# Gate/up weights of a decoder layer split four blocks at a time in place of two, and the first projection blocks in passes

## What is computed

```
h   = rmsnorm(x, attn_norm)
qkv = h @ w_in                          # 1024 x 3072
q, k = rope(q), rope(k);  two causal mixers of 8 heads each, side by side
mixed = [rmsnorm(o_moba, g1), rmsnorm(o_dil, g2)]
x = x + mixed @ w_out                   # 1024 x 1024
h = rmsnorm(x, ffn_norm)
g, u = h @ w_gate, h @ w_up             # 1024 x 2816 each
x = x + (silu(g) * u) @ w_down          # 2816 x 1024
return rmsnorm(x, final_norm)
```

## Time and profile before

| | us |
|---|---|
| median of 3 runs (lowest, highest) | 296.89 (296.17, 297.11) |
| profiled execution, its own time | 296.56 |
| its span (first to last instruction) | 294.7 |
| TensorE busy | 284.1 (96% of the span) |
| VectorE busy | 264.3 (90%) |
| ScalarE busy | 190.0 (64%) |

### The profile page before, as it was taken

How to read it: one execution, slowest core, us unless ns; L and a number is a source line. 1 busy time by engine, 2 the same in 40 slices (tenths; PEclk the granted TensorE clock), 3 DMA queues, 4 the chain that set the end, 5 groups by cost and what they waited for, 6 DMA issues and landing times.

```text
span 294.7 us, 4123 instructions
## 1 busy us (share of the span) xinstructions
PE 284.1 (96%) x1396; PEld 232.4 (79%) x1396; DVE 264.3 (90%) x424; ACT 190.0 (64%) x323; POOL 21.5 (7%) x27
## 2 busy tenths in 40 slices
PE   8899999999999999999999999999999999999990
PEld 4688878888888888888887888888888888888870
DVE  3788999999798869799899999999999999988993
ACT  3887767846696629867566674748484848475524
POOL 0002000000131514200000000000000000000040
PEclk9999999999999999999999999999999999999998
DMA  7999616797867828695766587777657483223003
GB/s 242 392 420 365 212 38 212 218 290 210 274 201 206 322 83 270 201 301 182 221 257 250 210 256 277 246 283 213 249 161 304 126 335 75 109 48 131 2 0 142
DMA packets 29797, 62.87 MB, mean 213 GB/s; under 512 B 3792, under 2 KB 17104, under 8 KB 28368
## 3 DMA queue, kind: packets, MB, share of 16 engines
q1 hardware_dynamic: 27616, 61.03, 60.5%
q10 hardware_dynamic: 2160, 1.59, 1.7%
HBM read 55.72 MB, written 1.11 MB: 193 GB/s over the span
## 4 chain that ended last, share of the span: by engine, by line
PE 79%; DVE 9%; DMA 3%; issue 3%; ACT 2%; SPq 1%; POOL 0%; POOLq 0%; ACTq 0%
PE bank L587 25%; PE bank L588 24%; PE bank L589 24%; PE bank L664 2%; DMA room<-in_first 2%; DVE w_lo L1366 2%; DMA room<-room 1%; SPq L494 1%; PE bank L614 1%; DVE room L1409 1%; DVE o_lo L1422 1%; PE bank L637 1%; ACT w_hi L1034 1%; DVE o_lo L1429 1%; PE bank L597 1%
## 5 line engine op out<-in xcount | busy, mean ns | idle before, releaser
L587 PE MATMUL bank<-w_hi,x_hi 128*128 128x512 f32 x230 | 91.1, 396 | 1.6 <-DVE w_lo L1236 1.4
L589 PE MATMUL bank<-w_hi,x_lo 128*128 128x512 f32 x230 | 89.6, 390 | 0.0
L588 PE MATMUL bank<-w_lo,x_hi 128*128 128x512 f32 x230 | 89.6, 389 | 0.0
L587 PEld LDWEIGHTS bank<-w_hi,x_hi 128*128 128x128 f32 x230 | 43.2, 188 | 12.0 <-DVE w_lo L1236 1.8
L589 PEld LDWEIGHTS bank<-w_hi,x_lo 128*128 128x128 f32 x230 | 43.2, 188 | 9.2
L588 PEld LDWEIGHTS bank<-w_lo,x_hi 128*128 128x128 f32 x230 | 43.2, 188 | 8.5
L901 ACT ACTIVATE w_hi<-raw 128x1024 fp32r<-128x1024 f32 x33 | 33.7, 1050 | 9.8 <-issue 9.6
L1208 DVE TENSOR_TENSOR w_lo<-raw,w_hi 128x1024 fp32r<-128x1024 f32 x32 | 38.3, 1211 | 1.2 <-ACT w_hi L901 1.1
L1366 DVE TENSOR_TENSOR w_lo<-raw,w_hi 128x1024 fp32r<-128x1024 f32 x30 | 36.2, 1216 | 0.4
L1034 ACT ACTIVATE w_hi<-raw 128x1024 fp32r<-128x1024 f32 x29 | 30.2, 1051 | 0.0
L1045 ACT ACTIVATE rope_b<-bank,rstd 128x256 f32<-128x256 f32 x22 | 10.4, 471 | 30.6 <-PE bank L589 30.4
(11 more groups left out here) (149 smaller groups left out, 478.3 us busy)
## 6 DMA issues: line engine op xcount, KB each, us to landing
raw<-in_weights SPq DMA_DIRECT2D x74, 512.0 KB, 5.5
room<-in_weights SPq DMA_DIRECT2D x10, 1024.0 KB, 6.7
room<-room SPq DMA_DIRECT2D x76, 64.0 KB, 2.2
room<-in_first SPq DMA_DIRECT2D x3, 384.0 KB, 5.6
room<-in_first SPq DMA_DIRECT2D x1, 1024.0 KB, 9.1
xs<-in_x SPq DMA_DIRECT2D x2, 512.0 KB, 9.7
rot<-turned_sums SPq DMA_DIRECT2D x8, 128.0 KB, 4.1
room<-room ACTq DMA_DIRECT2D x12, 64.0 KB, 2.6
```

The source lines that it names most:

```text
L587: pe.matmul(dst, a_hi, w1, start=first, stop=False)
L588: pe.matmul(dst, a_hi, w2, start=False, stop=False)
L589: return pe.matmul(dst, a_lo, w1, start=False, stop=last)
```

## The change

It has three parts.

1. The gains are appended to the first load, 24 words a partition, which moves to its own room. The load from ScalarE's queue is gone. VectorE's first x_hi reads them where they land; POOL copies them to `gain`, and VectorE's first x_lo and ScalarE wait for that copy.
2. `first_block` becomes `early_block`, used for the even ones of the first eight blocks: 0, 2, 4 and 6.
3. In the chunk steps 3 to 9, the gate/up blocks of chunks 4 to 10 are split four at a time: two instructions of 2048 columns a chunk on each engine in place of four of 1024. Each raises `hi_ready` or `lo_ready` by 2.

In the later steps the first half of the next chunk's weights also stands ahead of the first down parts as a whole, where before only one pair did. The diff, cut to its core:

```diff
@@ build, room for the first loads
         for row_blocks, blocks in FIRST_LOADS:
-            width = len(row_blocks) * SEQ + len(blocks) * NB
-            first_dst.append(room[:, word:word + width])
+            start = word = word if first_dst else FIRST_ROOM
...
+            if not first_dst:
+                first_gain = room[:, word:word + G_END]
+                word += G_END
+            first_dst.append(room[:, start:word])
+            if len(first_dst) == 1:
+                word = 0
@@ TensorE
-            def first_block():
...
+            def early_block(i):
+
+                j, k = QKV_ORDER[i]
+                pe.wait_ge(*((xt_hi, k) if k else (x0_hi, 1)))
+                pe.wait_ge(hi_single, i // 2 + 1)
                 for s in range(SH):
+                    pe.matmul(bank[2 * j + s][:], x_hi[:, k, s * P:(s + 1) * P], w_hi[:, i, :], start=k == 0, stop=False)
+                pe.wait_ge(xt_lo, k + 1)
                 for s in range(SH):
+                    pe.matmul(bank[2 * j + s][:], x_lo[:, k, s * P:(s + 1) * P], w_hi[:, i, :], start=False, stop=False)
+                pe.wait_ge(lo_single, i // 2 + 1)
                 for s in range(SH):
+                    ins = pe.matmul(bank[2 * j + s][:], x_hi[:, k, s * P:(s + 1) * P], w_lo[:, i, :], start=False,
+                                    stop=k == KT - 1)
                 ins.then_inc(blk_done, 1)
...
-                if i == 0:
-                    first_block()
+                if i < SINGLES and i % 2 == 0:
+                    early_block(i)
                     return
@@ ScalarE
-            act.dma_start(gain[:], gains[:, :]).then_inc(in_gain, 16)
...
+            def gate_up_hi_half(c, h):
+
+                for j in (2 * h, 2 * h + 1):
+                    act.wait_ge(raw_full[j], ring_loads(STEP1_PAIR + j) + 16 * (c - 1))
+                act.wait_ge(gu_done, 2 * c - 2)
+                at = slice(QUAD * h, QUAD * h + QUAD)
+                act.activation(gate_up_at(c, QUAD * h, QUAD)[0], raw[:, at, :], ACT.Copy).then_inc(hi_ready, 2)
...
                 if c < NCH - 1:
-                    gate_up_hi(c + 1, 0)
+                    gate_up_hi_half(c + 1, 0)
                 else:
                     last_down_hi(0)
                 if c > 3:
                     down_first_hi(c - 2, 0)
                     down_first_hi(c - 2, 1)
-                if c < NCH - 1:
-                    gate_up_hi(c + 1, 1)
-                else:
+                if c == NCH - 1:
                     down_second_hi(c - 2)
                 hidden_hi(c - 1)
-                if c < NCH - 1:
-                    gate_up_hi(c + 1, 2)
-                else:
+                if c == NCH - 1:
                     last_down_hi(1)
                 evacuate(c, 0)
                 hidden_sums_hi(c - 1)
                 if c < NCH - 1:
-                    gate_up_hi(c + 1, 3)
+                    gate_up_hi_half(c + 1, 1)
                     down_second_hi(c - 2)
@@ VectorE
             def first_lo(k):
 
                 dve.wait_ge(*((xt_hi, k) if k else (x0_hi, 1)))
+                if k == 0:
+                    dve.wait_ge(in_gain, 1)
...
-            dve.wait_ge(in_gain, 16)
             dve.wait_ge(in_first[0], 16)
-            dve.tensor_scalar(x_hi[:, 0, :], first_x[0], gain[:, G_ATTN:G_ATTN + 1], None, ALU.mult).then_inc(x0_hi, 1)
+            dve.tensor_scalar(x_hi[:, 0, :], first_x[0], first_gain[:, G_ATTN:G_ATTN + 1], None, ALU.mult).then_inc(x0_hi, 1)
...
+            def gate_up_lo_half(c, h):
+
+                dve.wait_ge(hi_ready, STEP1_PAIR + (c - 1) * G_PAIRS + 2 * h + 2)
+                hi, lo = gate_up_at(c, QUAD * h, QUAD)
+                dve.tensor_tensor(lo, raw[:, QUAD * h:QUAD * h + QUAD, :], hi.bitcast(f32),
+                                  ALU.subtract).then_inc(lo_ready, 2)
...
-                gate_up_lo(c + 1, 0)
+                gate_up_lo_half(c + 1, 0)
                 if c > 3:
                     down_first_lo(c - 2, 0)
                     down_first_lo(c - 2, 1)
-                gate_up_lo(c + 1, 1)
                 hidden_sums(c - 1)
-                gate_up_lo(c + 1, 2)
                 multiply(c, 0)
                 turn_squares(c, 0)
                 hidden_lo(c - 1)
-                gate_up_lo(c + 1, 3)
+                gate_up_lo_half(c + 1, 1)
                 down_second_lo(c - 2)
@@ POOL
+            pool.wait_ge(in_first[0], 16)
+            pool.tensor_copy(gain[:], first_gain).then_inc(in_gain, 1)
```

More of the change, by code:

```diff
@@ L126 @@
 FRONT_W = 480
+FIRST_ROOM = 11 * NB
 PE_PLAN = {
@@ L240, in attention_tile, with build @@
     return 1, [4 * (u - 1) + 2 * i + r for i in range(2)], SEQ
-def build(nc, x, first, weights, gains, final_norm, table, out):
+def build(nc, x, first, weights, final_norm, table, out):
     f32, f32r, bf16 = mybir.dt.float32, mybir.dt.float32r, mybir.dt.bfloat16
@@ L937, in _ @@
             split_single(1)
-            act.wait_ge(in_gain, 16)
+            act.wait_ge(in_gain, 1)
             for b in range(2, SINGLES):
@@ L1703 @@
     x_turned = x[0].T.reshape(KT, P, SEQ)
-    first = np.concatenate([np.concatenate([x_turned[k] for k in row_blocks] + [qkv[b] for b in blocks], axis=1).reshape(-1)
-                            for row_blocks, blocks in FIRST_LOADS])
     gains = np.concatenate([get[n].reshape(-1, P) for n in ("attn_norm", "moba_out_norm", "dil_out_norm",
                                                             "ffn_norm")]).T
+    first = np.concatenate([np.concatenate([x_turned[k] for k in row_blocks] + [qkv[b] for b in blocks]
+                                           + ([] if i else [gains]), axis=1).reshape(-1)
+                            for i, (row_blocks, blocks) in enumerate(FIRST_LOADS)])
     arrays, args = {}, []
-    for name, a in (("x", x), ("first", first), ("weights", np.stack(loads[FIRST_QUADS:])), ("gains", gains),
+    for name, a in (("x", x), ("first", first), ("weights", np.stack(loads[FIRST_QUADS:])),
                     ("final_norm", get["final_norm"]), ("table", table)):
```

9 lines of the change are left out of this document (1 added, 8 removed).

## The result

The changed kernel takes 297.54 us (median of 22 executions, 296.81 to 299.08), the kernel before 296.68 in 22 (295.65 to 297.26): ratio 1.0033, 95% interval 1.0021 to 1.0045. It is slower by a third of a per cent. The forecast of 297.0 was 0.5 us short. The time lies inside the range, but the most likely case, no difference, did not come: the ratio sits on the edge of what can be told. The profiled execution took 297.6 with a span of 295.8, against 296.56 and 294.7, so there are +1.1 us of span to explain. The ratios are estimated apart from the medians and are not always their quotient.

The account below looks back on a forecast made before the run. TensorE was taken as the bound; -0.1 (head) -0.3 (evacuation) +0.5 (down parts) +0 gave +0.1 us, so a 297.0 us median from 296.89. Range 295.9 to 298.5, the forecast's own 296.4 to 297.7.

Parts of the forecast that it names:

- Items 1 and 2: Head: gains in first load worth 0; early blocks in passes start block 3 0.77 us earlier, keeping 0.1 at block 8.
- Item 3: Step 3, ScalarE: evacuation done earlier, by 157.8, so TensorE's wait at 158.82 goes: -0.3 us.
- Item 4: Step 3, second half: VectorE idles 0.74 us, a new wait for ScalarE's 2048-wide w_hi.
- Item 5: Step 3, second down parts: w_lo late, TensorE waits, +0.5 us; items 3 to 5 together +0.2.
- Item 6: Steps 4 to 9: VectorE's cycle 15.55, 0.1 under TensorE's 15.64, so lateness does not grow; value 0.
- Item 7: SP's loads of pairs 2 and 3 leave together after the second half; DMA engines not full; value 0.
- Item 8: Last step: VectorE enters some 1.5 us later, but TensorE's end products have idle VectorE time ahead; 0, bound +0.5.
- A: Rival, steps 4 to 9: VectorE becomes the bound, cycle 15.94 over 15.64, time 299.1, or 298.0 with half; chance 0.22.
- B: Rival, head and chunks: last first load lands 0.65 sooner, both stalls go, none comes; -1.1, 295.8; chance 0.12.
- C: Rival: edits do not reach TensorE; head 0, evacuation and lateness cancel; 296.9; chance 0.66 together with the forecast.

Follow-up runs that it names:

- passes_only: Kernel before with only the pass-by-pass order of early blocks 0, 2, 4 and 6 on TensorE: 296.85 us, ratio 1.0002 to the kernel before.
- gains_only: Kernel before with only the gains appended to the first load: 296.54 us, ratio 0.9998 to the kernel before.
- second_in_pairs: Changed kernel with each chunk's second half as two 1024-wide splits on both engines, same new place: 296.72 us, ratio 1.0002 to the kernel before.
- Chunks_only: Kernel before with only the chunk-step edit, head as before: 297.49 us, ratio 1.0032 to the kernel before.
- down_load_first: Changed kernel with SP sending the down-weight load ahead of the next chunk's gate/up pairs 0 and 1: 297.33 us, ratio 1.0032 to the kernel before.
- first_in_pairs: Changed kernel with each chunk's first half in two pairs at their old places, second half still wide: 297.34 us, ratio 1.0017 to the kernel before.
- all_pairs_late: Changed kernel with every split in pairs, so only pair 2's later place differs from before: 296.25 us, ratio 0.9993 to the kernel before.

## Why the prediction was right in most of its mechanisms and short in its sum

**Items 1 and 2, the head (0, -0.1).** The mechanism held: the stall stands at 16.91, ahead of block 8, on VectorE's first 1024-wide w_lo. The trace shows -0.44, because the last first load was ready 0.31 earlier (11.89 against 12.20), and the restart kept 0.13; passes_only and gains_only, at 1.0002 and 0.9998, say that on average it is about nothing. The size of 0.77 for block 3's lead was a little high: four matmuls of 0.23 don't fit between the rounded w_hi, ready near 8.4, and the w_lo of 9.1. Passes_only shows 0.65, and the stall at 9.16 was no fixed feature of the kernel before.

**Item 3, the evacuation (-0.3).** It was done by 157.51, and the stall went. The ledger gives -0.48 from the start of step 3 to 158.34: the stall's gap, 158.24 to the second matmul at 159.16, is 0.92 where two pitches are 0.45. The stall's bracket of 0.19 counts only the time in which the last matmul had drained; starts have to be compared with starts.

**Item 4, the new wait (0.74).** Measured 0.70 to 0.72 ahead of each of seven second halves. The 2048-wide instructions cost 2.28 and 1.90, as the lines had it; the dear side, 2.35, was two in pairs, which second_in_pairs shows is what pairs still cost.

**Item 5, the down parts (+0.5).** A stall came where it was forecast, and at 164.55 the ledger stood at -0.07 against a forecast of +0.1. The stall is larger, +0.75, only because TensorE arrived earlier; head and evacuation gave more and all of it was taken back. A gain ahead of a place where VectorE is late anyway is worth nothing. That the ledger stands at -0.04 at the end of step 3, close to the +0.1 of the sum, is partly luck: three terms were larger than forecast and cancelled.

**Item 6, steps 4 to 9 (0): this step failed.** The cycle was forecast at 15.55 and is 15.56 where nothing else waits (167.45 to 183.01). From "under TensorE's 15.64" I concluded that no lateness grows, and gave it 0. TensorE's steps 4 to 9 took 0.88 more than before (94.72 against 93.84). The step went wrong in taking slack for something that only has to be above zero. VectorE leaves step 3 0.8 later than before (multiply at 167.45, before 166.66), of which 0.69 is the wait for the down load at 164.85. With 0.08 of slack it would work that off in ten steps, with 0.61 in two (an estimate). So it comes out as the stall at 180.36, and another such wait, 0.59 at 196.45, as that at 211.97. The cycles with such waits are 16.1 long (157.55 to 173.69, and 183.01 to 199.05 is 16.04). Chunks_only has the first of these waits and the first of these stalls, and neither of the second pair; down_load_first has neither wait and neither stall; second_in_pairs has the 0.71 and 0.65 of slack, and no stall.

**Item 7, the DMA queue (0).** The item named no late down load, and VectorE waited for two, 0.69 and 0.59, where before it waited for none in steps 3 to 9. As a price by itself its 0 was nearly right: down_load_first, with the load sent first, is no faster, and second_in_pairs bears the same late landing without loss. It is a cost only together with item 6, and I valued the two apart.

**Item 8, the end (0, bound +0.5).** +0.2: VectorE got on with the last down sums at 270.18, after 1.41 of waiting for their load, in place of 268.67 after 1.04. That what releases the load had moved back is the item's own reading; no run tests it.

**Sum.** -0.1 -0.3 +0.5 was +0.1. The ledger has -0.44 +0.10 (between head and step 3, not traced) -0.48 +0.78 (step 3) = -0.04, then +0.51 +0.36 +0.20 = +1.03. What was missing is the term after step 3, 0.87 of the 1.03, and the runs put it on the hand-over: with the second half in pairs it is gone. The time lies inside even the forecast's own range, up to 297.7, but no term of the sum led there.

**The rivals.** A was near: its place (steps 4 to 9), its loop and its sentence on the margin of 0.1 held, its price did not, since it had the cycle exceed 15.64. What happened is a case that I had not written down, between the forecast and A: a cycle just under the bound, with lateness that never comes off. B fell: the last first load lands no earlier for the gains' move. C held to the end of step 3, at -0.04, and fell after it.

The Trainium skill (Perfetto Trace Analysis, section "Optimizing Scalar/DVE Operations") was weighed in both its halves: group where the engine is saturated, break up where it is not and causes bubbles on others. The trace agrees with the second: VectorE was at 15.03 of 15.64, grouping cost 0.7 of waiting per chunk to save 0.1 of work, and breaking the second half up again took the loss away.

**What stays open.** Why down_load_first, with fewer late landings, isn't faster by a tenth or two was not settled; in its profile another late load took their place, and one profile doesn't tell whether the order of SP's loads causes it. Why the down load comes late in one execution and not in another was not tested. The chunk steps of before can be hit as well: the profile of gains_only has a TensorE stall of 1.06 in step 2 (147.43 to 148.72), ahead of second down parts, where VectorE's multiply came 0.7 later than in the profile of before. The difference between first_in_pairs and the changed kernel is within their intervals. Of the versions in pairs none can be told from the kernel before; the lowest ratio among them, 0.9993 of all_pairs_late, is 0.4% under that of the changed kernel.

## What to carry to other kernels

Two engines that hand a tile from one to the other work in pipeline only over pieces: joining the last pieces behind a dependence makes the second engine wait for the whole first instruction, here 0.70 us, for the saving of one fixed part, 0.1. Before an instruction is made wider, compare its full length on the producer with the work the consumer has in hand at that point. And where an engine's cycle comes out just under the bound, don't price it at nothing: its slack is what takes up late transfers, so ask in how many rounds a lateness of the usual size would be worked off.

## What the runs showed of the hardware

- Fixed part of wide instructions: 128x2048 took 2.28 us on VectorE and 1.90 on ScalarE, where two of 1024 in a row take 2.35 and 1.99. Fourteen instructions fewer on either engine are worth 1.9 us of busy time each in this trace, more than 7 x 2 x 0.1 = 1.4; the rest is unexplained.
- The last of the six first loads was ready between 11.50 and 12.82 us from the span's start in the profiles of these kernels, though its bytes are the same. Block 8's second matmul came 5.35 or 5.36 behind it in the twelve profiles in which TensorE had stopped for it, and 5.48 in that of before, where it had not, so this one landing moves the head by over a microsecond.
- The first load with 24 words more showed no price: ScalarE began on it at 3.57 to 3.92, without them at 3.61 to 3.85. With the gains apart VectorE started 0.17 to 0.21 behind ScalarE, with them at the same time, and nothing of it is in the time.
